# Odd attention of a streaming encoder: where the chunk mask of the diagonal block is added

## What is computed

```python
q, k, v = jnp.split(h @ w_in, 3, axis=-1)            # q, k: (B, T, 8, 2, 64) after rotary; v: (B, T, 8, 128)
kchunk = jnp.arange(P + T) // CHUNK                  # CHUNK = 64
s = jnp.einsum('bqhcd,bkhcd->bhcqk', qb, k_all)      # c = 0, 1: the two maps
s = jnp.where((qp // CHUNK)[:, None] >= kchunk[None, :], s, NEG_INF)
p = jax.nn.softmax(s, axis=-1)
a = p[:, :, 0] - lam * p[:, :, 1]
o = jnp.einsum('bhqk,bkhd->bqhd', a, v_all)
```

## Time and profile before

| | |
|---|---|
| median of three runs | 2608.28 us |
| profiled execution, its own time | 2615.28 us |
| profiled execution, span | 2613.2 us |
| mean granted TensorE clock | 0.972 |
| PE busy | 2454.7 us (94%) |
| VectorE busy | 1699.5 us (65%) |
| ScalarE busy | 1206.8 us (46%) |
| chain that ended last | PE 78%, VectorE 12%, ScalarE 4% |

### The profile page before, as it was taken

How to read it: one execution, slowest core, us unless ns; L and a number is a source line. 1 busy time by engine, 2 the same in 40 slices (tenths; PEclk the granted TensorE clock), 3 DMA queues, 4 the chain that set the end, 5 groups by cost and what they waited for, 6 DMA issues and landing times.

```text
span 2613.2 us, 37692 instructions
## 1 busy us (share of the span) xinstructions
PE 2454.7 (94%) x13907; PEld 2190.8 (84%) x13907; DVE 1699.5 (65%) x2809; ACT 1206.8 (46%) x2239; POOL 118.5 (5%) x177
## 2 busy tenths in 40 slices
PE   5999999998899899999989999999988898999998
PEld 5999987977767799988789998877777577999887
DVE  6777647676555877754687775474235858777546
ACT  5545435344344555543555553453224655554444
POOL 1000001100001000000100000010000010000000
PEclk9999999999899899999989999999997999999999
DMA  4233234421303232234522333343343042223335
GB/s 127 80 90 89 97 129 161 114 69 49 106 1 117 66 93 82 82 113 136 169 66 82 92 87 113 129 157 97 105 125 114 1 142 68 81 82 95 99 128 177
DMA packets 259140, 261.89 MB, mean 100 GB/s; under 512 B 25568, under 2 KB 214000, under 8 KB 258977
## 3 DMA queue, kind: packets, MB, share of 16 engines
q1 hardware_dynamic: 254224, 243.83, 31.1%
q0 software_dynamic: 4464, 14.80, 1.6%
q10 hardware_dynamic: 288, 1.10, 0.1%
HBM read 249.11 MB, written 10.58 MB: 99 GB/s over the span
## 4 chain that ended last, share of the span: by engine, by line
PE 78%; DVE 12%; ACT 4%; issue 3%; DMA 1%; POOL 1%; ACTq 0%; DVEq 0%; SPq 0%; POOLq 0%
PE ps L845 13%; PE ps L847 13%; PE ps L846 13%; PE ps L903 5%; PE ps L905 5%; PE ps L904 5%; PE ps L1311 3%; PE ps L1313 2%; PE ps L1312 2%; PE ps L962 2%; PE ps L964 2%; PE ps L963 2%; PE ps L1797 1%; PE ps L1501 1%; DVE xb L708 1%
## 5 line engine op out<-in xcount | busy, mean ns | idle before, releaser
L845 PE MATMUL ps<-xb,w_all 128*128 128x320 f32 x2400 | 752.3, 313 | 50.1 <-DVE w_all L592 29.4
L846 PE MATMUL ps<-xb,w_all 128*128 128x320 f32 x2400 | 749.0, 312 | 0.0
L847 PE MATMUL ps<-xb,w_all 128*128 128x320 f32 x2400 | 748.8, 312 | 0.0
L845 PEld LDWEIGHTS ps<-xb,w_all 128*128 128x128 f32 x2400 | 457.0, 190 | 58.3 <-issue 43.2
L492 DVE TENSOR_TENSOR w_all<-raw,w_all 128x1024 fp32r<-128x1024 f32 (+1 forms) x204 | 207.8, 1020 | 393.9 <-ACT w_all L502 212.6
L846 PEld LDWEIGHTS ps<-xb,w_all 128*128 128x128 f32 x2400 | 457.3, 191 | 0.0
L847 PEld LDWEIGHTS ps<-xb,w_all 128*128 128x128 f32 x2400 | 457.1, 190 | 0.0
L486 ACT ACTIVATE w_all<-raw 128x1024 fp32r<-128x1024 f32 (+1 forms) x204 | 182.4, 895 | 477.5 <-PE ps L905 254.8
L592 DVE TENSOR_TENSOR w_all<-raw,w_all 128x512 fp32r<-128x512 f32 x404 | 277.9, 690 | 147.1 <-ACT w_all L585 146.1
L585 ACT ACTIVATE w_all<-raw 128x512 fp32r<-128x512 f32 x404 | 253.2, 629 | 182.5 <-PE ps L847 139.2
L903 PE MATMUL ps<-w_all 128*128 128x512 f32 x528 | 205.9, 390 | 1.0 <-DVE w_all L507 1.0
(11 more groups left out here) (357 smaller groups left out, 3989.9 us busy)
## 6 DMA issues: line engine op xcount, KB each, us to landing
raw<-in_w_ffn_out SPq DMA_DIRECT2D x176, 512.0 KB, 3.4
raw<-in_w_ffn_in SPq DMA_DIRECT2D x120, 512.0 KB, 5.1
gain<-in_w_ffn_in SPq DMA_DIRECT2D x56, 512.0 KB, 5.0
raw<-in_w_in_odd SPq DMA_DIRECT2D x56, 256.0 KB, 2.7
raw<-in_w_out_even SPq DMA_DIRECT2D x16, 512.0 KB, 3.5
raw<-in_w_out_odd SPq DMA_DIRECT2D x16, 512.0 KB, 3.5
gain<-in_norm_g POOLq DMA_DIRECT2D x12, 512.0 KB, 7.3
raw<-in_w_in_even SPq DMA_DIRECT2D x24, 256.0 KB, 2.6
```

What stands on the lines that cost most here:

```text
L845: nc.tensor.matmul(dst, wl, xh[:, k, :], start=first, stop=False, skip_group_check=True)
L846: nc.tensor.matmul(dst, wh, xl[:, k, :], start=False, stop=False, skip_group_check=True)
L847: mm = nc.tensor.matmul(dst, wh, xh[:, k, :], start=False, stop=(k == HK - 1), skip_group_check=True)
```

## The change

The product of queries and keys is no longer closed. Behind it PE adds the mask by a second product into the same bank: the 64x64 corner of the identity as weights, the 64x64 corner of the mask as moving data, onto partitions 0 to 63 and the last 64 columns. VectorE's addition goes. `skip_group_check` only tells the builder that the second product covers a part of the first one's output. The signal `qk_mm` moves to the mask product of map 1.

```diff
-                            mm = nc.tensor.matmul(bank(sc_bank(n, odd) + m, w), qTO[64 * m:64 * m + 64, h, i * P:(i + 1) * P],
-                                                  kTO[64 * m:64 * m + 64, h, 0:w], start=True, stop=True)
+                            b = sc_bank(n, odd) + m
+                            nc.tensor.matmul(bank(b, w), qTO[64 * m:64 * m + 64, h, i * P:(i + 1) * P],
+                                             kTO[64 * m:64 * m + 64, h, 0:w], start=True, stop=False, skip_group_check=True)
+
+                            mm = nc.tensor.matmul(ps[0:CHUNK, b, i * P + CHUNK:w], ident[0:CHUNK, 0:CHUNK],
+                                                  con[0:CHUNK, C_NC + CHUNK:C_NC + P], start=False, stop=True,
+                                                  skip_group_check=True)
...
                 if odd:
                     b = sc_bank(n, odd)
-
-                    both = ps[0:CHUNK, b:b + 2, i * P + CHUNK:w]
-                    link(dve, nc.vector.tensor_tensor(both, both, con[0:CHUNK, C_NC + CHUNK:C_NC + P].unsqueeze(1)
-                                                      .to_broadcast([CHUNK, 2, P - CHUNK]), ALU.add))
                     nc.vector.tensor_reduce(rneg[:, :, r], ps[:, b:b + 2, 0:w], AX.X, ALU.max,
                                             negate=True).then_inc(s_ready, 1)
```

## The result

The changed kernel takes 2682.08 us (median of 4 runs, 2677.85 to 2683.8) against 2613.55 us before: ratio 1.0257, 95% interval 1.0239 to 1.0276, some 68 us slower. The forecast was 2638 us with a range up to 2662: the sign is right, the size is not.

What follows compares the result with a forecast made beforehand. PE and VectorE lead each other by little before; PE becomes the bound everywhere. Four groups sum to 114.2 us against 77.3, +36.9; corrections of about -1 and -5.7 leave +30, so 2638 us, 8-in-10 range 2603 to 2662.

Steps and rivals of the forecast that it cites:

- the bound and its direction: Odd attention: PE has only 0.3 to 0.5 us per step to give, so it becomes the bound everywhere.
- the broken pair: Odd attention on PE: mask 0 parts the two QK^T, adding one single QK^T per step, 0.49 to 1.12 us.
- a late hand-over at each of the four changes of shape: Within each odd-attention step on PE: every change of array shape drains, with only 0.07 us of overlap.
- the mask product: Two per odd-attention step on PE, priced at 0.40 us each, of which 0.07 overlap the operation before.
- the ceiling of 6.6 us: Odd attention: removing VectorE's mask additions is worth at most 5.9 us of chain plus 0.7 for gaps.
- the term for the granted clock: Odd attention: slow clock in the first group only, and half of that group at full clock, -5.7 us.
- the work: PE's steps in odd attention: 3.49, 2.83, 3.61 and 4.35 us by group, 114.2 us against 77.3, +36.9.
- Rival (c): Odd attention: PE stays at 1.2 GHz beyond the first group, the 256-wide group costing 15 us more: 2659; chance 0.10.

Runs made afterwards that it cites:

- one_shape_apart: Changed kernel's order QK, mask, QK, mask, with each mask product in its own QK^T's shape (64x128) and array half: 2611.58 us, ratio 0.9987.
- no_mask: Kernel before without VectorE's mask addition and with no mask in its place in odd attention: 2608.51 us, ratio 0.9974.
- after_filler8: Changed kernel plus one full-array product of 512 columns, read by nothing, in each of its first 8 steps: 2633.91 us, ratio 1.0082.
- after_filler: Changed kernel plus one full-array product of 512 columns, read by nothing, in each of its first 16 steps: 2642.8 us, ratio 1.0123.
- break_one: Changed kernel with mask 1 in QK^T's shape, mask 0 left at 64x64 between the two QK^T: 2679.83 us, ratio 1.0269.

## Why the prediction was wrong

**Right: the bound and its direction.** PE had too little slack and became the bound in every group; VectorE's relief vanished in waiting: in the 384-wide group it is busy 18.95 of 47.7 us, where it was 20.24 of 21.20.

**Right: the broken pair, and the shape as its cause.** A second QK^T of 1.12 us per step, a late hand-over at each of the four changes of shape, the mask product at 0.33 us (taken at 0.40): 4.10 us for 4.35. The page TensorEngine Tiling (Array Packing) of the Trainium skill says under Key Properties that a change of the tiling mode drains the engine, and that different tiles can load and multiply in parallel. The trace agrees with both: at the change of columns alone the load begins 0.07 us ahead of the end, and one_shape_apart has the two maps' products side by side in one mode., which I set against it, are fp32r products of 128 rows; whether the type, the rows or the 16 columns make the difference is not shown.

**Right: the ceiling of 6.6 us** for the removal (no_mask: 7).

**Wrong: the clock, a correction of the wrong sign.** The step that failed is the term for the granted clock. The sum took the slow clock for the first group only, as before, and even 5.7 us off, for "a PE without gaps may be granted the full clock sooner". A gapless PE was at 1.2 GHz for 129.7 us. The size of that step comes from after_filler8, whose groups behind the first are all at 2.4 GHz. Its 256-wide group holds three fillers of 0.86 us (the same 384-wide step takes 3.86 us with one in after_filler and 3.00 without in after_filler8), so its work is 22.8 - 2.6 = 20.2 us. The slow clock then cost 35.6 - 20.2, 47.7 - 26.2 and 39.2 - 27.8 = 15.4 + 21.5 + 11.4 = 48.3 us. By this estimate the changed kernel at the full clock behind its first group would be some 20 us above before; after_filler8, with 2.6 us of fillers in those groups and a first group as long as the changed kernel's, measures +23.5.

**Too dear: the work.** What is left, 67.9 - 48.3 = 19.6 us (8.1, 0.8, 5.0 and 5.7 by group; the 0.8 against a group that was itself at half clock for 8 of its 19.4 us before), is the work, where the sum without its correction for the clock had +36. By group it had 27.9, 22.6, 28.9 and 34.8 us; measured are 22.6 at the slow clock, and 20.2, 26.2 and 27.8 + 4.1 = 31.9 at the full one. The first group was dear by 5 us, four of them in its first three steps, which have no transposes or values yet: VectorE's reductions come 1.5, 2.2 and 2.7 us apart, then 3.1, where 3.49 was set for all. The others were dear by 2.4 to 2.9 us (at 512 columns 0.25 per step: mask 0.33 for 0.40, transposes and values 1.48 for 1.58; and the first three steps of each still carry narrower transposes and values). And 32 full steps were set against a stretch that holds 31 and the last QK^T, some 3 to 4 us too much. So the forecast came nearer to the measured time than its clock deserved: the dear work made up for a part of it.

Rival (c) had the mechanism and was given 0.10. Its 15 us for the 256-wide group are what the runs show, but it was priced for one group more (2659) where it held for two and a half. The evidence was there: in the earlier trace rows PE is busy 21.0 of 23.7 us at half clock, so being busy had not brought the clock up there; and a PE-bound stage pays for the slow clock, where VectorE's pace had hidden it. When a change makes PE the bound, the whole stage has to be priced at both clocks. Slow to its end, the 512-wide group would take 6.91, 6.91 and 7.13 us for its first three steps and 7.55 for each of the other four, 51.2 us against 27.8. That makes 15.4 + 21.5 + 23.4 = 60 us more, and a range up to 2608 + 20 + 60 = 2688 (an estimate from these traces).

**Open.** Why the full clock came at 2132 us in the changed kernel and not before, and what exactly holds it. In the changed pattern full-array fillers raised it within 3 to 7 us, and the pattern then kept it to the stage's end, up to 69 us after the last of them; yet the changed kernel had the full clock for its first 2.5 us and lost it, and regained it in the 512-wide group without help, as break_one did. The order QK, transposes, QK, values lost it again. The runs show these states, not the rule behind them.

## What to carry to other kernels

Two products on half of PE's rows run side by side only while nothing of another shape stands between them; before a small product is slipped in, look whether the records of its neighbours overlap, and give it their shape (weights padded with zeros) on their partitions. And price a step that will be PE-bound at both levels of the granted clock: a stretch that was slow and hidden is paid for once PE sets the pace. The addition on VectorE was worth 7 us at most here; its replacement cost ten times that.

## What the runs showed of the hardware beyond that

- More work made the kernel faster: with 8 full-array fp32 products of 512 columns it is 24 us above before instead of 68 (2634 us for 2682, each on its own chip; four of five executions).
- The same PE-bound pattern ran at 1.2 GHz for over 100 us in one kernel and at 2.4 GHz to the end in others (after_filler8: 69 us after its last filler). Which of the two it was followed what PE had executed before; fillers in four steps in the middle switched it.
- Within one shape the two maps' products, on different halves of the array, don't keep the list's order: the four weight loads of both QK^T are over in 0.31 us with a mask listed between them.
- Masks in QK^T's shape cost 0.33 us for both maps (one_shape_apart: 0.34), of which 0.18 us lie under the QK^T before; in 64x64 one of them costs 0.33.
